# A two-layer hybrid trunk with expert retrieval: U gathers and products lead V by 24 slots instead of 16

## What is computed

```python
def block(xb):                       # 128 tokens
    q = (xb @ w_q).reshape(tb, PEER_HEADS, 2, PEER_D_KEY // 2)
    s = jnp.einsum('thcd,hckd->thck', q, sub_keys, ...)
    top_s, top_i = lax.top_k(s, kk)
    ...
    best_s, best_pos = lax.top_k(cand.reshape(tb, PEER_HEADS, kk * kk), kk)
    expert = jnp.take_along_axis(...)
    gate = jax.nn.softmax(best_s, axis=-1)
    u = u_tab[expert]
    act = jax.nn.gelu(jnp.einsum('td,thkd->thk', xb, u, ...), approximate=False)
    w = (gate * act).astype(xb.dtype)
    return jnp.einsum('thk,thkd->td', w, v_tab[expert])
```

## Time and profile before

| | |
|---|---|
| median of three runs | 3370.0 us (3364.2 to 3380.0) |
| profiled execution | span 3366.8 us from the first to the last instruction; nothing is shown apart from the span for its own time |
| PE / DVE / POOL / ACT busy | 79% / 68% / 67% / 22% of the span |
| HBM traffic | 1181.5 MB read, 352 GB/s over the span |
| gathers | 2048, 1073.9 MB, 84.2% of the DMA engines' time |
| chain that ended last | POOL 27%, PE 23%, DVE 20%, issue 17%, DMA 11% |

### The profile page before, as it was taken

How to read it: one execution, slowest core, us unless ns; L and a number is a source line. 1 busy time by engine, 2 the same in 40 slices (tenths; PEclk the granted TensorE clock), 3 DMA queues, 4 the chain that set the end, 5 groups by cost and what they waited for, 6 DMA issues and landing times.

```text
span 3366.8 us, 25897 instructions
## 1 busy us (share of the span) xinstructions
PE 2658.0 (79%) x7200; PEld 1257.8 (37%) x7200; DVE 2274.4 (68%) x4952; ACT 737.2 (22%) x1644; POOL 2267.3 (67%) x2074
## 2 busy tenths in 40 slices
PE   7866778998888778987887868998888776666667
PEld 3444333444354333433344423334435332222222
DVE  1559964579579984668659994568758995455443
ACT  2411121223221121223221121223322111111111
POOL 0025677777766777777776677777776676777776
PEclk9888899999998899999999889999999898988989
DMA  5248999999999999999999899999999999999998
GB/s 185 75 172 301 345 345 408 406 405 368 361 388 351 379 341 400 407 407 362 350 396 381 325 361 384 405 406 393 358 389 368 335 328 350 346 370 371 368 362 332
DMA packets 351442, 1185.41 MB, mean 352 GB/s; under 512 B 37666, under 2 KB 38212, under 8 KB 351044
## 3 DMA queue, kind: packets, MB, share of 16 engines
q0 software_dynamic: 294912, 1073.87, 84.2%
q1 hardware_dynamic: 56388, 109.88, 8.9%
HBM read 1181.52 MB, written 2.10 MB: 352 GB/s over the span
## 4 chain that ended last, share of the span: by engine, by line
POOL 27%; PE 23%; DVE 20%; issue 17%; DMA 11%; another core or an unknown queue 1%; ACT 1%; DVEq 0%; POOLq 0%; ACTq 0%
POOL v_ring L468 13%; POOL u_ring L468 13%; PE peer_acc L1258 12%; DMA v_ring<-in_peer_v,experts 8%; PE act_bank L1045 5%; DVE u_ring L986 4%; DMA u_ring<-in_peer_u,experts 4%; PE dve_bank L1045 2%; DVE work L752 2%; DVE work L741 1%; DVE work L749 1%; DVE work L738 1%; DVE work L931 1%; DVE work L933 1%
## 5 line engine op out<-in xcount | busy, mean ns | idle before, releaser
L1258 PE MATMUL peer_acc<-v_ring,diag 128*128 128x512 f32 x3584 | 1805.4, 645 | 647.1 <-DMA v_ring<-in_peer_v,experts 296.7
L986 DVE SCALAR_TENSOR_TENSOR u_ring<-u_ring,h 128x1024 f32<-128x1024 f32 x1024 | 1255.2, 1226 | 841.2 <-DMA u_ring<-in_peer_u,experts 730.1
L468 POOL DMA_INDIRECT v_ring<-in_peer_v,experts x1024 | 1146.9, 1120 | 524.3 <-issue 259.6
L468 POOL DMA_INDIRECT u_ring<-in_peer_u,experts x1024 | 1114.9, 1089 | 561.2 <-issue 308.9
L1258 PEld LDWEIGHTS peer_acc<-v_ring,diag 128*128 128x128 f32 x3584 | 688.5, 203 | 1647.7 <-issue 1009.4
L669 ACT ACTIVATE diag<-ident,wts 128x128 f32<-128x128 f32 x896 | 325.8, 397 | 1180.5 <-PE peer_acc L1258 580.9
L1045 PE MATMUL act_bank<-w_ring,hT 128*128 128x512 f32 x768 | 346.4, 598 | 0.7 <-ACT hT L508 0.7
L1045 PEld LDWEIGHTS act_bank<-w_ring,hT 128*128 128x128 f32 x768 | 147.5, 193 | 187.0 <-issue 185.6
L996 DVE SCALAR_TENSOR_TENSOR xs<-v_ring,wts,xs 128x1024 f32<-128x1024 f32 x128 | 164.5, 1285 | 49.5 <-DMA v_ring<-in_peer_v,experts 40.0
L1132 PE MATMUL act_bank<-hT,w_ring 128*128 128x256 f32 x768 | 175.6, 384 | 0.0
L1132 PEld LDWEIGHTS act_bank<-hT,w_ring 128*128 128x128 f32 x768 | 148.6, 194 | 39.4 <-issue 20.9
(11 more groups left out here) (158 smaller groups left out, 1540.0 us busy)
## 6 DMA issues: line engine op xcount, KB each, us to landing
w_ring<-in_w_in SPq DMA_DIRECT2D x24, 2048.0 KB
w_ring<-in_peer_w_q SPq DMA_DIRECT2D x16, 2048.0 KB
w_ring<-in_w_out SPq DMA_DIRECT2D x8, 2048.0 KB
u_ring<-in_peer_u,experts POOLq DMA_INDIRECT x1024
v_ring<-in_peer_v,experts POOLq DMA_INDIRECT x1024
xs<-in_x SPq DMA_DIRECT2D x4, 512.0 KB, 7.2
keysT<-in_peer_sub_keys SPq DMA_DIRECT2D x2, 1024.0 KB
out<-xs SPq DMA_DIRECT2D x4, 512.0 KB
```

The costliest lines, as they stand in the source:

```text
L468: pool.indirect_dma_start(ring[:, n % depth, :], None, table, bass.IndirectOffsetOnAxis(ap=experts[:, tile % TILES, e:e + 1], axis=0),).th ...
L986: tell(nc.vector.scalar_tensor_tensor(out=row, in0=row, scalar=1.0, in1=h2[:, tile % TILES, :], op0=ALU.mult, op1=ALU.mult, accum_out=dots ...
L1258: ins = nc.tensor.matmul(peer_acc[:, j * 512:(j + 1) * 512], diag[:, (v_count(c, s) - 1) % DIAGS, :], v_ring[:, n % V_RING, j * 512:(j + 1 ...
```

## The change

It touches the order alone. `U_AHEAD` = 24: a U gather and its product stand 24 slots ahead of the V slot, not 16; before the first V slot come 24 U slots. `GELU_BEFORE` = 6: ACT's gelu of chunk c+1 stands at step 10 of chunk c. `WTS_BEFORE` = 3: DVE's weights of chunk c+1 stand at step 13 of chunk c. `add_tile` stays at step 0. `LEAD` goes from 10 to 24, so that the experts of a chunk are found in time for its earlier gathers. `h2`, which the U products read, is in SBUF before and after; rings, products, gathers and their number are the same.

```diff
--- before.py
+++ after.py
@@ -34,7 +34,10 @@
 ACT_BANKS = 3
 DVE_BANKS = 3
 V_EVERY = 8
-LEAD = 10
+LEAD = 24
+U_AHEAD = 24
+GELU_BEFORE = 6
+WTS_BEFORE = 3
 
 LOWEST = -3.0e38
 MASKED = -1.0e30
@@ -335,21 +338,24 @@
             mine = s // V_EVERY + 1
             return c * V_DVE + mine if by_vector(s) else c * V_PE + s + 1 - s // V_EVERY
 
-        def interleave(front, slot_u, slot_v, begin):
+        def interleave(front, slot_u, slot_v, begin, before, finish_tile):
 
 
             parts = (None for k in range(FRONTS) for _ in front(k))
             for _ in range(PARTS_ALONE):
                 next(parts)
-            for s in range(SLOTS):
-                slot_u(0, s)
+            for m in range(U_AHEAD):
+                slot_u(*divmod(m, SLOTS))
+            begin(0)
             done = 0
             for n in range(CHUNKS * SLOTS):
                 c, s = divmod(n, SLOTS)
-                if c + 1 < CHUNKS:
-                    slot_u(c + 1, s)
-                if s == 0:
-                    begin(c)
+                if n + U_AHEAD < CHUNKS * SLOTS:
+                    slot_u(*divmod(n + U_AHEAD, SLOTS))
+                if s == 0 and c % PH == 0 and c > 0:
+                    finish_tile(c // PH - 1)
+                if s == SLOTS - before and c + 1 < CHUNKS:
+                    begin(c + 1)
                 due = min(n + 1, LEAD) + (n + 1) * PARTS // (HALF * PH * SLOTS)
                 for _ in range(due - done):
                     next(parts, None)
@@ -470,24 +476,26 @@
                     bass.IndirectOffsetOnAxis(ap=experts[:, tile % TILES, e:e + 1], axis=0),
                 ).then_inc(landed[n % depth], 16)
 
-            for c in range(-1, CHUNKS):
-                if c + 1 < CHUNKS and (c + 1) % HPC == 0:
-                    k, part = divmod(c + 1, HALF * PH)
+            def gather_u(n):
+
+                c, s = divmod(n, SLOTS)
+                if s == 0 and c % HPC == 0:
+                    k, part = divmod(c, HALF * PH)
                     i, head = divmod(part, PH)
-
                     pool.wait_ge(routed, (k * QJ + head // HPC) * HALF + i + 1)
-                for s in range(SLOTS):
-                    if c + 1 < CHUNKS:
-                        n = (c + 1) * SLOTS + s
-                        if n >= U_RING:
-                            pool.wait_ge(u_used, n - U_RING + 1)
-                        gather(u_rows, u_ring, U_RING, u_landed, c + 1, s)
-                    if c >= 0:
-                        n = c * SLOTS + s
-                        if n >= V_RING:
-                            old_c, old_s = divmod(n - V_RING, SLOTS)
-                            pool.wait_ge(v_added if by_vector(old_s) else v_used, v_count(old_c, old_s))
-                        gather(v_rows, v_ring, V_RING, v_landed, c, s)
+                if n >= U_RING:
+                    pool.wait_ge(u_used, n - U_RING + 1)
+                gather(u_rows, u_ring, U_RING, u_landed, c, s)
+
+            for n in range(U_AHEAD):
+                gather_u(n)
+            for n in range(CHUNKS * SLOTS):
+                if n + U_AHEAD < CHUNKS * SLOTS:
+                    gather_u(n + U_AHEAD)
+                if n >= V_RING:
+                    old_c, old_s = divmod(n - V_RING, SLOTS)
+                    pool.wait_ge(v_added if by_vector(old_s) else v_used, v_count(old_c, old_s))
+                gather(v_rows, v_ring, V_RING, v_landed, *divmod(n, SLOTS))
 
 
         @block.scalar
@@ -669,7 +677,7 @@
                 nc.scalar.activation(diag[:, n % DIAGS, :], ident[:], ACT.Copy,
                                      scale=wts[:, c % 2, s:s + 1]).then_inc(diag_ready, 1)
 
-            interleave(front, lambda c, s: None, slot_v, begin)
+            interleave(front, lambda c, s: None, slot_v, begin, GELU_BEFORE, lambda tile: None)
 
 
         @block.vector
@@ -972,8 +980,6 @@
                 tell(nc.vector.tensor_tensor(v, v, peer_acc[:], ALU.add), peer_added, "peer_added")
 
             def begin(c):
-                if c % PH == 0 and c > 0:
-                    add_tile(c // PH - 1)
                 tile, head = divmod(c, PH)
                 dve.wait_ge(act_ready, c + 1)
                 tell(nc.vector.tensor_tensor(wts[:, c % 2, :], acts[:, c % 2, :], gates[:, tile % TILES, head, :],
@@ -997,7 +1003,7 @@
                                                     scalar=wts[:, c % 2, s:s + 1], in1=v,
                                                     op0=ALU.mult, op1=ALU.add), v_added, "v_added")
 
-            interleave(front, slot_u, slot_v, begin)
+            interleave(front, slot_u, slot_v, begin, WTS_BEFORE, add_tile)
             add_tile(LAYERS * TILES - 1)
 
 
@@ -1260,7 +1266,7 @@
                                            start=(e == 0), stop=last)
                 ins.then_inc(v_used, 1)
 
-            interleave(front, lambda c, s: None, slot_v, lambda c: None)
+            interleave(front, lambda c, s: None, slot_v, lambda c: None, 1, lambda tile: None)
 
 
 # ---- launch: one core; inputs and outputs as the reference has them ----
```

## The result

| | before | changed |
|---|---|---|
| median of 8 runs each, us | 3370.99 | 3391.55 |
| lowest to highest | 3356.53 to 3379.97 | 3387.36 to 3401.62 |
| profiled execution: time, span | span 3366.8 | 3401.62, 3399.8 |

The ratio is 1.0065 with a 95% interval of 1.0044 to 1.0086: some 21 us slower. The forecast was 3357 us. The time lies inside the stated range, on the side of rival C. V slot n is issued where the n-th gather of V (counted from 0) starts on POOL.

What follows compares the result with a forecast made beforehand. DVE was taken to bound the start and routing stages, full DMA engines and then POOL's issue pace the middle. Costs of +38 and gains of -51 gave -13 us: span 3354, median 3357 us, range 3295 to 3405.

Steps and rivals of the forecast that it cites:

- rival C: Start (V slots 0 to 47) is paid, nothing returns; decides if under 21 us come back; 3400 us, chance 0.19.
- Eight U slots alone: Before the first V slot: eight more U slots at 1.47 us each, +12 us.
- LEAD 24: V slots 0 to 47: all 35 routing parts crowd into steps 0 to 22 on DVE, +37 us.
- Eight more V slots alone: At the end: 24 V slots alone instead of 16, at 1.72 instead of 2.84 us, -9 us.
- Gelu and weights apart: At chunk boundaries: PE has work while ACT waits, so the boundary wait should go; together -51 us.
- the -27 us of the middle stages: Three middle stages: a third of the 78 us that POOL waits there comes back.
- The -14 of the routing stages: Routing stages: of at most 21 us of DVE's unbusy time, including the first U gather's wait for `routed`, 14 return.
- the -10 of the last stage: Last stage: of POOL's 15.6 us of waits for "remote", 10 of at most 14 come back.
- the forecast's -51: Sum of the gains in middle, routing and last stages, with ends of 0 and -113 us.
- Rival D: Boundary wait is moved to ACT's gelu at step 10, not removed; some crowding hides; about 3370 us, chance 0.14.
- Rival B: POOL's issues keep the faster phase against U products and waits go; 3295 us, up to 55 more; chance 0.17.

Runs made afterwards that it cites:

- the crowded kernel: The changed kernel itself, with its extra front parts all at the start: 3391.55 us; with gelu and weights back at the boundary 3396.59 us.
- the spread one: Changed kernel with 14 extra front parts due one every four slots from V slot 47: 3366.76 us; with gelu and weights back at the boundary 3370.11 us.
- The dose on POOL: Kernel before with a small memset on POOL, and POOL's wait for it, ahead of each gather: 3447.87 us, ratio 1.0235.
- the balanced pair: Kernel before (U 16 ahead) and changed kernel (U 24 ahead), both with a table spreading routing parts over more slots: 3335.71 and 3328.74 us.

## Why the prediction was wrong

**The two costs at the start were right.** Eight U slots alone: +12 forecast; the first V gather is issued at 261 us instead of 251, +10, and +8 to +13 in the experiments with U 24 ahead. LEAD 24: +37 forecast, +34 measured by itself at V slot 48. Together: 49 forecast, 55 found, and 48 and 52 in the two kernels that differ only in the place of gelu and weights. The forecast gave slot 48 as 443 us before and 490 after; 443 is where the stage ends on DVE, while POOL issues the slot at 427 and 482, so the shift was right and the place was not. The forecast also left out the wait of U slot 32 for `routed` (28.53 us), with V slot 8 behind it. It held that this signal now comes earlier than it is needed. For the three later fronts that is so, and their 15 us of such waits are gone; at the start it comes earlier, and is needed earlier still, because U is 24 ahead.

**The end was right.** Eight more V slots alone: -9 forecast, -9 found (from slot 1000 to the last, 42 us behind become 33).

**The step that failed is "Gelu and weights apart", the -27 us of the middle stages first.** It took a third of the 78 us that POOL waits for PE there as recoverable. The middle stages came out at 531, 533, 538 us against 528, 534, 526: nothing recovered, and POOL's waits for PE in the first of them are 31.9 us, not a third less than 26.7. With the wait put back the total is 2 to 5 us higher in the crowded kernel and 3 to 6 in the spread one. In the three middle stages PE's waits for diagonals fell from 58 to 35 us, and 28 us of waits for the tile sum, one in each stage, took their place; no run moved the tile sum. But what paces a slot is mostly neither: POOL needs 1.12 + 1.09 + 0.60 = 2.81 of a slot's 2.92 us whatever PE waits for. The forecast had this number, and named the full DMA engines as the limit beside it, but then still gave a third of a wait back. The dose on POOL and the kernel without the weights' bytes speak for the other order of the two: 29 GB/s taken off are worth 6 us a stage at the most, while 0.09 us more per gather lengthen it by a third to two thirds of the dose, 11 to 20 us.

**The -14 of the routing stages and the -10 of the last stage had about the right size, for a reason that the runs do not bear out.** The routing windows are shorter by 24 us, 10 of them because they hold fewer slots, and V slots 816 to 1000 take 526 us instead of 535, although POOL's "remote" waits in the last stage grew from 15.6 to 25.9. But LEAD 24 alone, with U 16 ahead, has all 24 of the first and 7 of the 9 of the second. It is the shift of the parts that does it, and the middle windows, which hold as many V gathers as before, are 14 us longer together and take it back.

Put together in the profiled executions: 55 us at the start, -4 over the middle and routing stages, -9 in the last stage and -9 in the V-only end are the 33 between the last V issues, of which some 12 are the draw of that execution. So of the forecast's -51 this execution has 13, and LEAD alone has 14. By the medians, which are 21 us apart, some 25 of the 55 us came back before the V-only end, and some 10 of the 34 with LEAD alone. What U's distance and the early weights gave behind slot 48, the end apart, is thus between nothing and some 15 us, and these runs do not settle it; in the balanced pair the distance and the early weights brought 14 us back on the way. The middle windows show none of the -27.

Rival C had the right mechanism for the middle and the right point of decision: the time is 21 us up and not 38, so by the forecast's own costs 17 came back, fewer than its 21. Its 3400 us are 8 above what was measured, and they contain a -8 for which the forecast gives no row. Rival D's "moved, not removed" applies at tile boundaries, where PE's wait moved from the weights to the tile sum. Rival B, the free pace, showed a trace of itself: U's issues on POOL fell from 1089 to 1053 ns on average (1061 with LEAD 24 alone), 36 us over the kernel, and U's waits for DVE rose by 41, from 18.9 to 59.8 us.

**What stays open.** That a slot takes 2.92 and not POOL's 2.81 us, and that some 26 us of waits in a middle stage survive each change of rings, bytes and boundary, has not been explained; only the dose on POOL took them away, and the stage became longer. Why DVE waits 3 to 4 us in a routing stage with the shifted parts instead of 7 to 14 was not tried; the waits of POOL for `routed` that are gone from these stages are a candidate. The worth of U's distance in the balanced schedule, some 7 us net, is smaller than these runs can settle.

## What to carry to other kernels

A wait on an engine that is not the pacer is slack, not loss: ask before crediting it what the pacing engine needs per unit of work (here POOL, 2.81 of 2.92 us), and take the difference between the two as the most that can come back, which another wait may still claim. Here that most was 20 us a stage; the forecast took 9 of it, and even these did not come, so the difference is a bound and not a price. A prologue that crowds the work of one engine leaves the others idle for as long as the crowding lasts (here POOL was busy 54 of 157 us); spreading the same work to where that engine has idle time was worth more than the longer lead of the queue. Follow the lead slot by slot to the end before booking such a gain: here most of what a stage won was paid back in the next one, and what remained was the part after which no busy stage followed. To learn whether a wait matters, put it back into the changed kernel, or lengthen the ring that it hangs on: if the wait changes its name and the total stays, there was little to win.

## What the runs showed of the hardware

The DMA share stands at 1.00 in a middle stage with 386 GB/s, and at 0.96 with 357, over the same number of gathers: here a full share did not mean that the bytes bind. Nor does it say how much more could be moved: 0.99 went with 371 GB/s and 1.03 with 406, held for 240 us.

The Trainium skill, "DMA: Bandwidth & Descriptors", section "Where 436 GB/s comes from", gives about 358 GB/s a core from HBM as what binds, worked out as half of what a pair of cores shares; here one core runs. By that the kernel without the weights' bytes should have run faster by the 15 MB of each middle stage. It sits at 357 GB/s there without a gain, which looks like that figure, but the kernel before moves 386 in the same time, so the trace does not agree that it is the limit.

A 128x8 memset on POOL takes 0.12 us and POOL's own wait for it 0.27, and yet the two add only 0.09 us between two gathers (0.30 to 0.39).

POOL's mean of 1.09 to 1.12 us for a gather is not what a gather takes alone, 0.94. In the kernel before, between 440 and 3340 us, the 63 gathers that begin in the first 0.2 us of a U product of DVE take 1.73 us on average, the 89 that begin 0.6 to 0.8 us into it 1.33, and the 442 that begin in its last 0.2 us 0.97; a gather already under way when a product starts takes 0.94 to 0.96 when the product follows within 0.4 us. At 0.94 for each, a slot would cost POOL 2.48 us instead of 2.81 (an estimate from these rows). No run here tried to keep the two apart.
